# A three-branch transformer kernel: in its second block's feed-forward one chunk of down weights is held back, and the last two are multiplied together

## What is computed

```python
def conv_glu_ffn(x, w_up, conv_w, conv_b, w_down):
    h = x @ w_up
    hp = jnp.pad(h, ((0, 0), (1, 1), (0, 0)))
    h = hp[:, :-2] * conv_w[0] + hp[:, 1:-1] * conv_w[1] + hp[:, 2:] * conv_w[2] + conv_b
    a, b = jnp.split(h, 2, axis=-1)
    return (jax.nn.gelu(a) * b) @ w_down

def second_block(x, p, ...):
    for i in range(DEPTH):
        ...
        ffn = conv_glu_ffn(x, w_up[i], conv_w[i], conv_b[i], w_down[i])
        ple = jax.nn.sigmoid(x @ w_ple_gate[i]) * (p[i] @ w_ple_proj[i])
        x = layer_norm(DEEPNORM_ALPHA * x + ffn + ple, ln2_g[i], ln2_b[i])
    return x
```

## Time and profile before

| | |
|---|---|
| Median of 3 runs | 1954.64 us (1953.98 to 1955.01) |
| Profiled execution, its own time | 1954.63 us |
| Its span, first to last instruction | 1952.8 us |
| PE busy | 1940.7 us, 99% |
| DVE busy | 1363.1 us, 70% |
| ACT busy | 1035.5 us, 53% |
| HBM read | 359.40 MB |
| Granted clock of TensorE, mean | 0.999 |

### The profile page before, as it was taken

One profiled execution on the slowest core, in us unless ns is written; L12 is line 12 of the kernel. 1 busy time (PEld: TensorE's weight loads), 2 busy tenths in 40 slices (PEclk: granted clock), 3 DMA queues, 4 the chain that ended last, 5 costly groups with the idle time before them and its releaser, 6 DMA issues.

```text
span 1952.8 us, 27601 instructions
## 1 busy us (share of the span) xinstructions
PE 1940.7 (99%) x10534; PEld 1665.2 (85%) x10534; DVE 1363.1 (70%) x1652; ACT 1035.5 (53%) x1201; POOL 164.3 (8%) x152
## 2 busy tenths in 40 slices
PE   9999999999999999999999999999999999999998
PEld 8888978888888889788889978888888978888887
DVE  7666577666676666677666556577888666677887
ACT  6444555544454455655445554356556554456664
POOL 0000130000000003104002201040001301000000
PEclk9999999999999999999999999999999999999999
DMA  8555635455455546456555544564554554555552
GB/s 328 193 185 180 206 140 194 174 192 193 172 194 193 193 160 207 153 179 234 186 191 190 171 178 141 206 248 176 193 193 145 196 177 158 208 206 191 186 191 87
DMA packets 55132, 365.74 MB, mean 187 GB/s; under 512 B 6672, under 2 KB 7952, under 8 KB 12176
## 3 DMA queue, kind: packets, MB, share of 16 engines
q1 hardware_dynamic: 49680, 349.99, 50.2%
q0 software_dynamic: 1472, 9.44, 1.3%
q10 hardware_dynamic: 3904, 5.25, 1.0%
HBM read 359.40 MB, written 1.05 MB: 185 GB/s over the span
## 4 chain that ended last, share of the span: by engine, by line
PE 96%; DVE 2%; ACT 1%; DMA 1%; issue 0%; ACTq 0%; SPq 0%; DVEq 0%
PE gate_two L1693 12%; PE up_two L1693 12%; PE bank L1624 9%; PE bank L1625 9%; PE bank L1626 9%; PE gate_two L1624 8%; PE gate_two L1626 8%; PE gate_two L1625 8%; PE gate_two L1698 6%; PE up_two L1698 6%; PE up_two L1882 1%; PE bank L1851 1%; PE up_two L1866 1%; PE bank L2143 1%; DVE w_lo L1019 0%
## 5 line engine op out<-in xcount | busy, mean ns | idle before, releaser
L1019 DVE TENSOR_TENSOR w_lo<-raw,w_hi 128x2048 fp32r<-128x2048 f32 x318 | 735.0, 2312 | 246.4 <-ACT w_hi L569 240.8
L569 ACT ACTIVATE w_hi<-raw 128x2048 fp32r<-128x2048 f32 x322 | 614.6, 1909 | 95.2 <-PE bank L1626 65.5
L1693 PE MATMUL gate_two<-br_parts,w_hi 128*128 128x512 f32 x1056 | 266.5, 391 | 0.9 <-DVE w_lo L1206 0.8
L1693 PE MATMUL up_two<-br_parts,w_hi 128*128 128x512 f32 x1024 | 246.2, 391 | 0.0
L1693 PEld LDWEIGHTS gate_two<-br_parts,w_hi 128*128 128x128 f32 x1056 | 198.1, 188 | 43.3 <-issue 2.0
L1693 PEld LDWEIGHTS up_two<-br_parts,w_hi 128*128 128x128 f32 x1024 | 188.2, 188 | 37.0
L1624 PE MATMUL bank<-w_lo,hid_hi 128*128 128x512 f32 x480 | 187.5, 391 | 0.0
L1625 PE MATMUL bank<-w_hi,hid_lo 128*128 128x512 f32 x480 | 187.5, 391 | 0.0
L1626 PE MATMUL bank<-w_hi,hid_hi 128*128 128x512 f32 x480 | 186.7, 389 | 0.0
L1624 PE MATMUL gate_two<-w_lo,br_parts 128*128 128x512 f32 x448 | 179.6, 401 | 0.0
L1626 PE MATMUL gate_two<-w_hi,br_parts 128*128 128x512 f32 x448 | 174.8, 390 | 0.0
(11 more groups left out here) (274 smaller groups left out, 2958.8 us busy)
## 6 DMA issues: line engine op xcount, KB each, us to landing
raw<-stream SPq DMA_DIRECT2D x328, 1024.0 KB, 4.8
area<-rpb POOLq DMA_DIRECT2D x2, 1536.0 KB, 7.8
area<-rows POOLq DMA_DIRECT2D x3, 1024.0 KB, 5.1
raw<-stream SPq DMA_DIRECT2D x8, 256.0 KB, 7.4
softT<-area ACTq DMA_DIRECT2D x32, 64.0 KB, 5.2
area<-rows POOLq DMA_DIRECT2D x2, 768.0 KB, 4.7
konst<-consts SPq DMA_DIRECT2D x1, 1344.0 KB, 9.0
area<-xT ACTq DMA_DIRECT2D x4, 256.0 KB, 6.7
```

Source lines behind the costliest of these rows:

```text
L569: act.activation(w_hi[:, s, :], raw[:, s, :], ACT.Copy).then_inc(hi_ready[s], 1)
L1019: dve.tensor_tensor(w_lo[:, s, :], raw[:, s, :], w_hi[:, s, :].bitcast(F32), ALU.subtract).then_inc(lo_ready[s], 1)
L1693: pe.matmul(pair[:, f, :, :], w_hi[:, s, at:at + P], parts[:, :, k, :], start=k == 0, stop=False, skip_group_check=True)
```

## The change

In the second block alone, `ffn_walk` is called with `held=1`. The loop has seven turns, and its tail is A9 B9 A10 B10 D8 D9 D10, so that D8 comes behind B10. The stream's chunks are laid out in that order. D9 and D10 are one piece of work, `second_final`: for each of the four banks PE does D9's six matmuls and then D10's six. `hidden` of index 9 goes to the other half of `att_hi` and `att_lo`, since index 8 still stands in `hid_hi` and `hid_lo`. B10 is multiplied by `halves` like the others, and summed. The eighth piece of the residual is prepared in A9's step. ACT splits the next layer's second chunk after it has normalized the first token half, since D9's weights are now used until shortly before the end. In the last layer ACT issues the third of the four transfers out.

```diff
-def ffn_walk(eng, c0, step):
+def ffn_walk(eng, c0, step, held=0):
     for n, (kind, i) in enumerate((("A", 0), ("B", 0), ("A", 1), ("B", 1), ("D", 0))):
         step(kind, i, c0 + n, 0)
-    with eng.Fori(0, PAIRS - 3) as turn:
+    with eng.Fori(0, PAIRS - 3 - held) as turn:
         for n, (kind, lag) in enumerate((("A", 0), ("B", 0), ("D", 1))):
             step(kind, turn + (2 - lag), c0 + 5 + n, turn)
-    for n, (kind, lag) in enumerate((("A", 0), ("B", 0), ("D", 1))):
-        step(kind, PAIRS - 1 - lag, c0 + FFN_CHUNKS - 4 + n, 0)
-    step("D", PAIRS - 1, c0 + FFN_CHUNKS - 1, 0)
+    last = [(kind, PAIRS - 1 - held + n) for n in range(1 + held) for kind in "AB"]
+    last += [("D", PAIRS - 2 - held + n) for n in range(2 + held)]
+    for n, (kind, i) in enumerate(last):
+        step(kind, i, c0 + FFN_CHUNKS - len(last) + n, 0)
...
-            for j in range(HALVES):
+            for j in (0, 1, 3):
                 sp.wait_ge(out_pair[j], 2)
                 sp.dma_start(out[:, j * 2 * T:(j + 1) * 2 * T], flat(work[:, 2 * j:2 * j + 2, :])).then_inc(out_done, 16)
...
-                        if c == CHUNKS[1] - 3:
-                            whole = banks[6]
-                        else:
-                            lower_half(up_other, up_two).then_inc(up_part.sem, 1)
-                            split_after(here, c, turn)
-                            act.wait_ge(up_sum.sem, here.at(up_sum, i + 1))
+                        lower_half(up_other, up_two).then_inc(up_part.sem, 1)
+                        split_after(here, c, turn)
+                        act.wait_ge(up_sum.sem, here.at(up_sum, i + 1))
...
+                        if c == CHUNKS[1] - 6:
+                            hidden_upper(here, PAIRS - 2, att_hi[:, 2:4, :])
+                        if c == CHUNKS[1] - 4:
                             hidden_upper(here, PAIRS - 1, att_hi)
-                    if kind == "D" and c < CHUNKS[1] - 2:
+                    if kind == "D" and c < CHUNKS[1] - 3:
                         hidden_upper(here, i + 1)
...
-                ffn_walk(act, MIX2, step)
+                    if c == CHUNKS[1] - 3 and layer < DEPTH - 1:
+                        split_after(here, c, turn)
+                ffn_walk(act, MIX2, step, held=1)
                 normed(1, 0)
+                if layer < DEPTH - 1:
+                    chunk_done(here, CHUNKS[1] - 2)
+                    split_after(here, CHUNKS[1] - 2)
                 normed(1, 1, (1,))
...
+            act.wait_ge(out_pair[2], 2)
+            act.dma_start(out[:, 4 * T:6 * T], flat(work[:, 4:6, :])).then_inc(out_done, 16)
...
+                        if c == CHUNKS[1] - 6:
+                            hidden_lower(here, PAIRS - 2, att_hi[:, 2:4, :], att_lo[:, 2:4, :])
+                        if c == CHUNKS[1] - 4:
                             hidden_lower(here, PAIRS - 1, att_hi, att_lo)
...
                             if j == 1:
                                 moments(1, 0)
-                            elif j == 2:
                                 away(1, 0)
...
-                    if c == MIX2 + 7:
-
-                        cols = bass.ds(turn * P, P)
+                    if c in (MIX2 + 7, CHUNKS[1] - 7):
+                        piece_of = turn if c == MIX2 + 7 else DT - 1
+                        cols = bass.ds(piece_of * P, P)
...
             def second_final(here, c):
 
-                def done(j, e):
-                    e.then_inc(acc_done.sem if j < HALVES - 1 else w_used[c % SLOTS], 1)
-                wide_down(c, att_hi, att_lo, fresh=False, last=done, order=(0, 2, 1, 3))
+                take(here, c - 1)
+                pe.wait_ge(hid_ready.sem, here.at(hid_ready, PAIRS - 1))
+                for n, j in enumerate((0, 2, 1, 3)):
+                    rows, out = slice(j % 2 * P, (j % 2 + 1) * P), flat(banks[j][:, :, :])
+                    for late in range(2):
+                        s = (c - 1 + late) % SLOTS
+                        if late and not n:
+                            take(here, c)
+                            pe.wait_ge(hid_ready.sem, here.at(hid_ready, PAIRS))
+                        for k in range(2):
+                            cols, t = slice(k * D + j // 2 * 2 * T, k * D + (j // 2 + 1) * 2 * T), 2 - 2 * late + k
+                            e = product(out, att_hi[:, t, rows], att_lo[:, t, rows], w_hi[:, s, cols], w_lo[:, s, cols],
+                                        start=False, stop=late == 1 and k == 1)
+                        if not late and n == HALVES - 1:
+                            e.then_inc(w_used[s], 1)
+                    e.then_inc(acc_done.sem if n < HALVES - 1 else w_used[c % SLOTS], 1)
...
-                        if here.kind == 1 and c == c0 + FFN_CHUNKS - 3:
-                            features(c, two(banks[6]), br_hi, br_lo, DT)
-                        else:
-                            halves(c, gate_two if kind == "A" else up_two, parts)
-                ffn_walk(pe, c0, step)
+                        halves(c, gate_two if kind == "A" else up_two, parts)
+                ffn_walk(pe, c0, step, held=here.kind)
```

More of the change, by code:

```diff
@@ L977, in step @@
                             add = cur[:, bass.ds(i * 2 + (C_CONVB + FT // 2 + a), 1)]
-                            e = act.activation(glu_b[:, a, :], whole[:, a, :], ACT.Identity, bias=add, scale=mid)
+                            e = act.activation(glu_b[:, a, :], up_other[:, a, :], ACT.Identity, bias=add, scale=mid)
                         e.then_inc(up_mid.sem, 1)
@@ L1549, in step @@
                     if kind == "B":
[L1550 to L1557 removed]
+                        dve.wait_ge(up_part.sem, here.at(up_part, i + 1))
+                        add_upper(up_other, up_two).then_inc(up_sum.sem, 1)
+                        split_after(here, c, turn)
+                        dve.wait_ge(up_sum.sem, here.at(up_sum, i + 1))
                         dve.wait_ge(up_mid.sem, here.at(up_mid, i + 1))
[L1559 removed]
+                        taps(glu_b, up_other, i, C_TAP + FT // 2, up_left, up_taps, i + 1)
                         dve.wait_ge(up_taps.sem, here.at(up_taps, i + 1))
@@ L1596, in step @@
                             e.then_inc(base_step.sem, 1)
-                        dve.wait_ge(base_step.sem, here.at(base_step, turn * 2 + 2))
+                        dve.wait_ge(base_step.sem, here.at(base_step, piece_of * 2 + 2))
                         dve.tensor_tensor(part, part, extra, ALU.add).then_inc(base_ready.sem, 1)
-                ffn_walk(dve, MIX2, step)
+                ffn_walk(dve, MIX2, step, held=1)
                 away(1, 1)
@@ L1749, in wide_whole, with wide_down @@
                 return e.then_inc(w_used[s], 1)
-            def wide_down(c, hi, lo, fresh, last=None, order=range(HALVES)):
+            def wide_down(c, hi, lo, fresh, last=None):
                 s = c % SLOTS
-                for n, j in enumerate(order):
+                for j in range(HALVES):
                     rows = slice(j % 2 * P, (j % 2 + 1) * P)
@@ L1761, in wide_down @@
                     if last:
-                        last(n, e)
+                        last(j, e)
                 return e.then_inc(w_used[s], 1) if last is None else e
@@ L1825, in step @@
                         if c == c0 + FFN_CHUNKS - 1:
-                            if here.kind == 0:
-                                hybrid_final(here, c, f)
-                            else:
-                                second_final(here, c)
+                            hybrid_final(here, c, f)
                         else:
@@ L2211, in _tile, with _ffn_chunks @@
     return part.reshape(-1, P, part.shape[1]).transpose(1, 0, 2).reshape(P, -1)
-def _ffn_chunks(up, down):
+def _ffn_chunks(up, down, held=0):
     whole = slice(None)
@@ L2223, in _ffn_chunks @@
     order = [("A", 0), ("B", 0)]
-    for i in range(1, PAIRS):
+    for i in range(1, PAIRS - 1 - held):
         order += [("A", i), ("B", i), ("D", i - 1)]
-    return [piece(*o) for o in order + [("D", PAIRS - 1)]]
+    order += [(kind, i) for i in range(PAIRS - 1 - held, PAIRS) for kind in "AB"]
+    order += [("D", i) for i in range(PAIRS - 2 - held, PAIRS)]
+    return [piece(*o) for o in order]
 def _columns(w, n, first=0):
```

33 lines of the change are left out of this document (8 added, 25 removed).

## The result

| | before | after |
|---|---|---|
| Median, run beside each other | 1954.74 us (1953.98 to 1956.14, 6 runs) | 1964.34 us (1961.37 to 1964.68, 6 runs) |
| Profiled execution, span | 1952.8 us | 1962.6 us |
| PE busy | 1940.7 us | 1945.3 us |
| Granted clock, mean | 0.999 | 0.997 |

The changed kernel is slower by a ratio of 1.0044 (95% interval 1.0033 to 1.0055). The forecast was 1963.7 us, in a range of 1960.2 to 1967.0. The median lies in it, and so does the profiled execution (1964.36). Two of the six executions took 1961.37 and 1962.01 us, at a mean clock of 0.998 instead of 0.997.

A forecast was written before the change was run, and what follows sets the result against it. The prediction took PE's matmul stream (99% busy) and the short DVE, POOL and ACT chain behind each D10 as the bound. It summed 1954.63 + 7.58 (layer ends) - 0.1 (transfer) + 1.55 (clock) = 1963.7 us, range 1960.2 to 1967.0.

The forecast's parts named there:

- PE's timetable: Second block's tail: PE reaches its wait for index 10's hidden values 29.06 us after A9's first matmul, after six D9 matmuls.
- DVE late at A9's sum (8.04): DVE starts A9's gate sum at 8.04 us, though PE ended A9 at 5.54; D7's step is unchanged, so this holds.
- When index 10 is ready (33.51): DVE's and ACT's steps from A9's sum, laid end to end, finish index 10's hidden values at 33.51 us.
- The wait: PE waits from 29.06 to 33.51 for index 10's hidden values, about 4.4 us in each layer.
- ACT's hold (1.04): In A10's step ACT's copy stands behind its wait for the product, delaying DVE's split from 21.48 to 22.52: 1.04 us.
- The end of a layer: Fourth sum starts 0.50 us behind the last matmul's start, at 43.36; losses of 3.90 and 3.68, together 7.58 us.
- The clock: Behind the new wait PE's clock falls to half pace in one of two layers, costing 1.55 us.
- The rival with two falls (1965.2): The clock falls behind the wait in both layers, +3.1 us instead of +1.55, giving 1965.2 us; chance 0.25.
- the forecast's case: The wait in both layers with one fall of the clock, 1963.7 us; chance 0.40.
- The transfer: At the kernel's end ACT's issue of one transfer out runs beside SP's: -0.1 us.
- ACT's split behind the first token half: At a layer's end, ACT's 1.90 us split hides before the second half's normalization; without cover it costs up to 1.9.
- Losses of 7.58 + 1.55: Both layers' later fourth sums, 7.58 us net of gains, plus one fall of the clock, 1.55 us.

The follow-up runs named there:

- the execution of 1962.67 us: One profiled execution of the changed kernel with all four transfers out issued by SP; timed later, that kernel had a median of 1964.89 us, ratio 1.005.

## Why the prediction was right, and where it was not

The total is right to 0.7 us. Two of its terms were off, in opposite directions, so the number is better than the sum behind it.

- **PE's timetable**: right. It put PE at the wait 29.06 behind A9's start; by the trace it was 29.07.
- **DVE late at A9's sum (8.04)**: right, 8.01. The change left this step as it was, and index 10's chain is laid end to end from it.
- **When index 10 is ready (33.51)**: 0.95 too late; it was 32.56, and PE resumed at 32.71. Each step was taken from rows 4, all of the loop. In the tail the same steps come sooner: taps to the next sum 1.70 instead of 1.82 (twice), the residual piece 1.13 instead of 1.25, taps to the upper part 2.55 instead of 2.72 (twice), `hid_hi` to DVE's split 2.95 instead of 3.07, `hid_hi` to the lower part 0.66 instead of 0.74, the start 0.03. Together 0.93. The durations are the same, the distances are not. One of these is no matter of the loop: to `hid_hi` and DVE's split the prediction laid ACT's copy with its full 0.60, where in the trace of before the next instruction already starts 0.50 behind the copy's start (1909.25 and 1909.75). The trace of before also had the unrolled distances: from B10's taps to the upper part 2.54 (1932.71 to 1935.25).
- **The wait**: 3.64 us instead of 4.4 a layer (PE's idle time of 3.48 and its start again); this term of the sum was mis-sized, by 0.8 twice. The experiments show that the wait is real and is this chain: it shrank with the hold gone (to 1.9), with the sum of B10 gone (to 2.7), with 42 matmuls in front of it instead of 30 (to 0.8), and was away altogether with 42 and no hold, or with 48.
- **ACT's hold (1.04)**: the idle piece was there, 1.00. That its removal would bring only this was wrong: 1.6 of wait, since DVE's idle piece for `att_hi` went with it.
- **The end of a layer**: right. The fourth sum stands 0.43 behind the last matmul's start (0.50 said). That D10's banks now come 2.7 us apart is worth 0.45 in the last layer (0.43 behind, where the kernel with D9 whole and `away(1, 0)` in its old place has 0.90 and the kernel before 0.88) and 0.66 in the first (0.44 and, before, 1.10).
- **The clock**: the term that was mis-sized. One fall at 1.55 was counted; in the profiled execution it fell in both layers, and cost 1.66 and 2.76. The rival with two falls (1965.2) had the number of falls right for it, but not their price (3.1 instead of 4.4). What neither had is that the executions of one kernel differ: with the same wait, one more trace shows a single fall of 1.65, which is the forecast's case nearly to the tenth, and one shows two falls, of 2.83 and 2.88. The two executions of 1961.37 and 1962.01, at 0.998, are likely of the first kind; they were not profiled. By the rule of the Trainium skill ("TensorE: Matmul & The Clock Gate", section "HAM oscillation — how this bites in real kernels"), a burst behind a long wait starts at the low clock. In the last layer the trace agrees, with 0.50. In the first it does not quite: four matmuls ran at full pace before the fall. And in the execution of 1962.67 us the first layer contradicts it: the burst ran at 1.00 from its start to its end.
- **The transfer**: -0.1 said, -0.08 in the profile's tail, and nothing that the runs can tell.
- **ACT's split behind the first token half**: hidden, as said. It becomes a cost of 0.65 in the kernel with D9 whole and `away(1, 0)` in its old place.

Losses of 7.58 + 1.55 = 9.13 were forecast and 10.27 measured; the first layer's earlier start of 0.42 brings the total closer still. So the total is partly luck: the wait was overestimated by 1.6, the clock underestimated by 2.9 in this execution.

## What to carry over

When work is moved so that an engine reaches a wait sooner, lay the waited-for chain end to end from the last point where it is already late; busy shares (DVE at 70%) say nothing of it. Distances from start to start read in a loop may be a tenth of a microsecond too long for unrolled steps, and over eight steps that counts. A wait of a few microseconds on TensorE should be priced twice, once as itself and once as the half pace behind it, in every place where it occurs, and the second price as a range: behind this kernel's wait it was nothing once and up to 2.9 us otherwise, and a single trace does not show the spread. Small matmuls put into it give back the second price, and an order of work that needs no wait gives back both.

## What the runs showed of the hardware

- **The clock fell behind idle times from 1.9 us on, and not always.** 1.75 us (`halves` in the kernel before): it held in both layers. 1.9 us (without the hold): it fell in the first layer and held in the last, in one profiled execution. 2.1 and 2.6 us, in the first layer's norm: it fell, though there PE has more short waits close by. 2.7 and 2.6 us (B10 by `features`): it held, in the fastest execution. 3.5 us (three traces of the changed kernel's PE program): it fell five times and held once. So the length of the wait alone did not decide here, and the same wait in the same kernel went either way; what decides is open.
- **The fall can come during the wait or after it**: at 0.50 from the first matmul in the last layer, four matmuls after resuming in the first. The matmuls ran slowly for about 3.1 us in the first layer (1492.2 to 1495.3) and for 5.7 in the last, at 0.43 us from matmul to matmul instead of 0.228. Each costs about half of its length, and all the prices read behind the wait lie near one of the two: 1.65 and 1.66 (also without the hold), or 2.76 to 2.88.
- **Twelve small matmuls were enough to hold it**, although PE still waited 0.8 us a layer behind them: in both layers of one trace, and by the mean clocks in all seven executions.
- **In the loop, DVE's and ACT's same steps come 0.08 to 0.17 us later from start to start** than in the unrolled tail, at equal durations. That the loop's addresses come from registers may be the reason; no run tested it. For the residual piece it is not: before the change the loop's last turn has 1.14 us from it to the next sum (1926.87 to 1928.01), with addresses from a register as in the turns ahead of it, which have 1.25. All of the 0.11 lies between its last instruction and the sum (0.35 and 0.46), the place where in the other turns the loop turns back.
